# Leaving out identity products that TensorE runs while it waits

## The chip, the cores and the metric

One core of one Trainium2 chip runs the whole program. The metric is the device time of one execution in microseconds (us); the change is judged by the median over several executions. A profile is one further execution, recorded by the hardware profiler.

## What is computed

Two blocks of two layers each work on 256 tokens of width 1024, all in float32. The second block has an even layer (a recurrent mixer) and an odd layer (attention and a state-space part), and each of them ends in a mixture of experts, the part that the change touches:

```python
def hier_moe(h, w_group, b_group, w_expert, b_expert, w_gate, w_up, w_down):
    g_logits = (hf @ w_group + b_group).astype(jnp.float32)
    g_prob = jax.nn.softmax(g_logits, axis=-1)
    g_top = jnp.argmax(g_logits, axis=-1).astype(jnp.int32)
    ...
    top_p, top_j = lax.top_k(e_prob, MOE_TOP_K)
    gates = g_w[:, None] * top_p / jnp.sum(top_p, axis=-1, keepdims=True)
    expert_idx = g_top[:, None] * MOE_EXPERTS_PER_GROUP + top_j.astype(jnp.int32)
    y = routed_experts(hf, expert_idx, gates, w_gate, w_up, w_down)
```

There are 32 experts in 4 groups of 8. Each token takes its best group and the two best experts in it. An expert computes `(silu(x @ w_gate) * (x @ w_up)) @ w_down` with a hidden width of 512. No product of the identity with itself is part of any of this.

## The kernel before

**Layout.** The 256 tokens are two tiles of 128. The weights of all 32 experts are read from device memory in each of the two layers: 16 pairs of experts per layer, a pair in six pieces of 2 MB (four quarters of gate and up, two halves of down). A pair's products hold 32 slots per expert; four of these 32-column products lie side by side in TensorE's array.

**Routing** (class `Router`). TensorE transposes x (`x_transposes`, L2853) and forms the logits (`logits`, L2862). VectorE picks group and experts for one tile at a time (`select`, L2768 to L2778; its last instruction, L2778, raises `s_sel`). In `ranks` TensorE multiplies a triangular matrix and a matrix of ones with the selections, to give each token its slot (L2873, L2874, L2877, L2878, L2879; 32 columns each). VectorE makes the rank of a tile from that (L2806) and then the gathering matrix (L3078), which opens the experts.

**Experts** (`expert_functions`). For the first pair TensorE gathers x by quarters of the width (`gather_first`, L3168), VectorE scales what was gathered (L3100), and TensorE multiplies a quarter (`gate_up`, L3190). The first two gather quarters stand ahead of the first `gate_up`, and each of the other two stands behind one. In the steady loop `of_pair` one pair follows another: four `gate_up`, transposes, the gather of the next pair (L3157), a turn of the hidden values (L3227), two `down` (L3204), and the products that put the results back to their tokens (L3238). The last pair is written out in `of_last`.

**Loads.** SyncE issues every transfer into one queue, and before each one it waits until the buffer is free. The loads of the third pair (L2967) wait for `s_gu` of the first pair: when the first `gate_up` is through, the buffer of the first quarter may be filled again. In the even layer a half piece (`part_of`, L2710, 1 MB) goes out first on that signal, and the first whole piece on the signal of the second `gate_up`. In the odd layer a whole piece goes out on the first signal. What was issued ahead of that is limited: in the odd layer the last loads before routing ends are those at L2256 and one of 1 MB at L2710.

**The identity products.** `keep_clock(pe, n)` (L2841 to L2845) issues n products of the 128x128 identity with itself into bank 7, where nobody reads them. It waits for nothing and signals nothing. It is called at four places:
- in `ranks`, 5 products ahead of the wait for the second tile's selection (L2875), in both layers;
- in `ranks`, 2 products at its end (L2880), in both layers;
- in `of_last`, 4 products ahead of the first `down` of the last pair, in the odd layer only (L3278); the even layer has the products L3249 there, which it needs;
- at the end of the even layer's experts, 3 products (L3301), behind the first transposes of the odd layer (L425) and ahead of that layer's first products (L2512).

TensorE works through its instructions in program order. The profile shows two records for each float32 product, so 5 products are 10 records.

Of the kernel before, what the change touches and what calls it, by code (L numbers as in the profile page):

```python
# [13 lines left out]
P = 128  # L14
# [2639 lines left out]
class Router:  # L2654
# [183 lines left out]
        link(dve, dve.tensor_tensor(self.oh2, self.oh2, u2(c2(316)), ALU.mult))  # L2838
        link(dve, dve.tensor_tensor(self.gate, self.oh1, self.oh2, ALU.add))

    def keep_clock(self, pe, n):  # L2841

        ident = self.g.con("ident")
        for _ in range(n):
            pe.matmul(self.g.ps[7][:, 0:P], ident, ident, start=True, stop=True)  # L2845

    def x_transposes(self, pe, tt, ch):
        pe.wait_ge(self.s_x, 2 * tt + ch + 1)
        if tt:
            pe.wait_ge(self.s_xT, ch + 1)  # L2850
        for kk in range(4):
            k = 4 * ch + kk
            ins = pe.transpose(self.g.ps[6 + ch][:, kk * P:(kk + 1) * P], self.g.x[:, tt, k * P:(k + 1) * P], self.g.con("ident"))  # L2853
        ins.then_inc(self.s_tr, 1)
# [11 lines left out]
    def ranks(self, pe):  # L2866
        g, ps, sel = self.g, self.g.ps, self.sel
        before, ones = g.con("before"), g.con("ones")
        of_tile = lambda tt: ps[tt][:, 0:NE]
        pe.wait_ge(self.s_xT, 4)  # L2870
        pe.wait_ge(self.s_lo, 1)
        pe.wait_ge(self.s_sel, 1)
        pe.matmul(of_tile(0), before, sel[:, 0, :], start=True, stop=True).then_inc(self.s_rk, 1)  # L2873
        pe.matmul(of_tile(1), ones, sel[:, 0, :], start=True, stop=False)  # L2874
        self.keep_clock(pe, 5)  # L2875
        pe.wait_ge(self.s_sel, TT)
        pe.matmul(of_tile(1), before, sel[:, 1, :], start=False, stop=True).then_inc(self.s_rk, 1)  # L2877
        pe.matmul(ps[2][:, 0:NE], ones, sel[:, 0, :], start=True, stop=False)  # L2878
        pe.matmul(ps[2][:, 0:NE], ones, sel[:, 1, :], start=False, stop=True).then_inc(self.s_rk, 1)  # L2879
        self.keep_clock(pe, 2)  # L2880


class Experts:
# [6 lines left out]
def expert_functions(g, ly, c0, router):  # L2890
# [5 lines left out]
    ident = g.con("ident")  # L2896
# [255 lines left out]
    def tensor(pe):  # L3152
# [28 lines left out]
        def gate_up(quarter, where, bank, rounds):  # L3181
            if rounds is None:
                arrived_early(bank, quarter)
            else:
                arrived(bank, quarter, rounds)
            for k in range(2):
                for which in range(2):
                    for e in range(2):
                        q = (2 * which + e) * CAP
                        ins = pe.matmul(b_gu[q:q + CAP, :], xg[:, 2 * quarter + k, e * CAP:(e + 1) * CAP],  # L3190
                                        up_w(where, quarter, e)[:, which, k, :], start=(quarter == 0 and k == 0),
                                        stop=(quarter == 3 and k == 1), tile_position=(0, q))
            ins.then_inc(s_gu, 1)
# [59 lines left out]
        def of_last(pairs, rounds):  # L3253
            for quarter in range(4):
                if quarter % 2 == 0:
                    pe.wait_ge(s_xg, pairs * 2)
                gate_up(quarter, later[1], 1, rounds)
                if quarter < 3:
                    add_x(quarter)
            pe.wait_ge(s_P, pairs * 2)  # L3260
            for tt in range(TT):
                ins = pe.transpose(b_t[:, S + tt * P:S + (tt + 1) * P], Pg[:, tt].rearrange("p h e j -> p (h e j)"), ident)
            ins.then_inc(s_Pt, 1)
            pe.matmul(b_x[:, 0:1], ident, ident[:, 0:1], start=True, stop=True).then_inc(s_G, 2)
            pe.wait_ge(s_PTc, pairs)
            add_x(3)
            pe.wait_ge(s_h, pairs)
            for f in range(4):
                turn = pe.matmul if f == 0 else pe.transpose
                ins = turn(b_t[:, f * 2 * CAP:(f + 1) * 2 * CAP], hid[0:2 * CAP, f * P:(f + 1) * P],  # L3270
                           ident[0:2 * CAP, 0:2 * CAP])
            ins.then_inc(s_ht, 1)
            pe.wait_ge(s_xg, pairs * 2 + 2)
            pe.wait_ge(s_hc, pairs)
            if ly == 0:
                K_products(g.s5)
            else:
                router.keep_clock(pe, 4)  # L3278
            down(0, later[1], 1, rounds).then_inc(s_da, 1)
            down(1, later[1], 1, rounds).then_inc(s_dn, 1)  # L3280
            pe.wait_ge(s_yc, pairs)
            for tt in range(TT):
                for nh in range(2):
                    r = slice(nh * 2 * CAP, (nh + 1) * 2 * CAP)
                    pe.matmul(ps[2 * tt + nh][:, :], PT[r, tt * P:(tt + 1) * P], y[r, :], start=False, stop=True,  # L3285
                              skip_group_check=True).then_inc(s_sum[2 * tt + nh], 1)
# [11 lines left out]
        if ly == 0:  # L3298
            for ch in range(2):
                g.n_odd.transpose_half(pe, 0, ch)  # L3300
            router.keep_clock(pe, 3)  # L3301

    return sync, scalar, vector, tensor, gpsimd if ly == 0 else None


# [123 lines left out]
```

## Time and profile before

| | us |
|---|---|
| median of 3 runs | 1538.08 (1537.22 to 1539.68) |
| profiled execution, own time | 1537.3 |
| its span, first to last instruction | 1535.4 |
| TensorE busy | 1292.0 (84%) |
| VectorE busy | 462.7 (30%) |
| ScalarE busy | 278.2 (18%) |
| GpSimd busy | 266.0 (17%) |

The mean rate of the transfers is 324 GB/s over the span. The experts of the even layer run from about 538 to 970 us of the span, those of the odd layer from about 1104 us to the end. The page gives shares of engines over the span, and in its second part the span in 40 slices of 38.4 us with the granted clock of TensorE and what the DMA engines moved. Stages with different limits stand in one share, so the stretch around each edit has to be read by itself.

### The profile page before, as it was taken

How to read it: one execution, taken by the hardware profiler on the slowest of the kernel's cores; microseconds unless marked ns; L12 is line 12 of the kernel's file. 1: busy time of each engine (PE TensorE's matmuls, PEld its weight loads, DVE VectorE, ACT ScalarE, POOL GpSimd, SP SyncE). 2: the span in 40 equal slices, each digit the busy share in tenths (PEclk: the TensorE clock that was granted, in tenths of full speed). 3: DMA queues.
4: the chain of work that ended last, by engine and by line, in shares of the span. 5: the costliest groups of instructions: out<-in, count | busy, mean ns of one | idle time of the engine just before them, and what ended most of it. 6: DMA issues, size and time to landing. Idle time of an engine off the chain costs nothing. (4 is left out here: it accounts for less than half of the span.)

```text
span 1535.4 us, 21931 instructions
## 1 busy us (share of the span) xinstructions
PE 1292.0 (84%) x9264; PEld 698.4 (45%) x9264; DVE 462.7 (30%) x903; ACT 278.2 (18%) x547; POOL 266.0 (17%) x158
## 2 busy tenths in 40 slices
PE   9999999999999999667767667999998776676666
PEld 5754466547878554223223322755544232232232
DVE  2554662654845531111000101286311010010011
ACT  2042410423322210300000000115211101011011
POOL 0676226641000008790000000000000000000000
PEclk9999999999999999888889999999999888999999
DMA  9932452336430699999999999946799999999997
GB/s 371 359 127 82 182 227 84 140 138 271 183 139 31 255 416 423 428 432 433 428 433 426 436 429 427 394 166 241 275 424 431 428 435 430 427 434 430 427 436 300
DMA packets 36514, 498.18 MB, mean 324 GB/s; under 512 B 5728, under 2 KB 8544, under 8 KB 12256
## 3 DMA queue, kind: packets, MB, share of 16 engines
q1 hardware_dynamic: 36448, 497.22, 77.9%
q8 instruction: 51, 0.84, 0.2%
q14 instruction: 15, 0.12, 0.0%
HBM read 495.11 MB, written 2.10 MB: 324 GB/s over the span
## 5 line engine op out<-in xcount | busy, mean ns | idle before, releaser
L3190 PE MATMUL banks<-weight_ring,spare_weights_arena 128*32 128x512 f32 x1472 | 220.9, 751 | 143.9 <-DMA weight_ring<-in_moe_weights 142.4
L3111 DVE TENSOR_TENSOR spare_weights_arena<-spare_weights_arena,banks 64x512 f32<-64x512 f32 x32 | 22.1, 690 | 658.5 <-ACT spare_weights_arena L3030 658.5
L3190 PEld LDWEIGHTS banks<-weight_ring,spare_weights_arena 128*32 128x32 f32 x1472 | 56.4, 132 | 297.5 <-issue 244.6
L3157 PE MATMUL banks<-spare_weights_arena,x 128*128 128x64 f32 x960 | 110.8, 274 | 0.0
L3157 PEld LDWEIGHTS banks<-spare_weights_arena,x 128*128 128x128 f32 x960 | 109.9, 192 | 0.0
L3030 ACT ACTIVATE spare_weights_arena<-banks 64x512 f32<-64x512 f32 x32 | 18.9, 591 | 501.8 <-PE banks L3190 501.8
L3204 PE MATMUL banks<-weight_ring,spare_weights_arena 128*32 128x512 f32 x728 | 89.4, 624 | 13.9 <-issue 7.6
L1001 POOL TENSOR_TENSOR weight_ring<-spare_weights_arena,weight_ring 128x2048 f32<-128x2048 f32 x16 | 74.0, 4638 | 70.9 <-DVE spare_weights_arena L845 38.5
L1114 PE MATMUL banks<-weight_ring,x_normed_hT_mix 128*128 128x512 f32 x192 | 84.7, 592 | 0.0
L3238 PE MATMUL banks<-spare_weights_arena 64*128 64x512 f32 x240 | 59.6, 615 | 20.9 <-ACT spare_weights_arena L3036 20.9
L338 PE MATMUL banks<-weight_ring,x_normed_hT_mix 128*128 128x512 f32 x128 | 56.3, 595 | 0.0
L1082 PE MATMUL banks<-x_normed_hT_mix,weight_ring 128*128 128x256 f32 x256 | 56.0, 379 | 0.0
L3190 PE MATMUL banks<-x_normed_hT_mix,spare_weights_arena 128*32 128x512 f32 x272 | 36.7, 669 | 22.1 <-DMA x_normed_hT_mix<-in_moe_weights 22.1
L1114 PEld LDWEIGHTS banks<-weight_ring,x_normed_hT_mix 128*128 128x128 f32 x192 | 35.7, 190 | 41.4 <-issue 41.3
L3204 PEld LDWEIGHTS banks<-weight_ring,spare_weights_arena 128*32 128x32 f32 x728 | 25.7, 113 | 57.6 <-issue 37.1
L1082 PEld LDWEIGHTS banks<-x_normed_hT_mix,weight_ring 128*128 128x128 f32 x256 | 48.4, 190 | 7.6 <-issue 1.2
L1001 POOL TENSOR_TENSOR weight_ring<-weight_ring 128x512 f32<-128x512 f32 (+1 forms) x14 | 37.9, 2726 | 80.5 <-DMA weight_ring<-in_ring_weights 73.5
L3238 PEld LDWEIGHTS banks<-spare_weights_arena 64*128 64x128 f32 x240 | 20.6, 186 | 62.3 <-ACT spare_weights_arena L3036 48.1
L3092 DVE TENSOR_TENSOR spare_weights_arena<-banks,spare_weights_arena 128x256 f32<-128x256 f32 x64 | 27.0, 424 | 62.8 <-PE banks L3157 62.7
L3190 PE MATMUL banks<-spare_weights_arena 128*32 128x512 f32 x304 | 34.7, 595 | 12.9 <-DMA spare_weights_arena<-in_moe_weights 12.9
L3036 ACT COPY spare_weights_arena<-banks 128x512 f32<-128x512 f32 x32 | 18.8, 586 | 137.1 <-PE banks L3204 137.1
L1088 PE MATMUL banks<-weight_ring,x_normed_hT_mix 128*128 128x512 f32 x96 | 41.8, 593 | 0.2 <-DVE x_normed_hT_mix L415 0.2
(557 smaller groups left out, 1823.7 us busy)
## 6 DMA issues: line engine op xcount, KB each, us to landing
weight_ring<-in_moe_weights SPq DMA_DIRECT2D x42, 4096.0 KB, 26.9
weight_ring<-in_moe_weights SPq DMA_DIRECT2D x53, 2048.0 KB, 19.0
weight_ring<-in_ring_weights SPq DMA_DIRECT2D x35, 2048.0 KB, 12.2
spare_weights_arena<-in_moe_weights SPq DMA_DIRECT2D x21, 2048.0 KB, 51.5
x_normed_hT_mix<-in_moe_weights SPq DMA_DIRECT2D x16, 2048.0 KB, 54.8
spare_weights_arena<-in_moe_weights SPq DMA_DIRECT2D x7, 4096.0 KB, 54.5
weight_ring<-in_ring_weights SPq DMA_DIRECT2D x4, 1024.0 KB, 6.0
x_normed_hT_mix<-in_moe_weights SPq DMA_DIRECT2D x4, 1024.0 KB, 4.9
```

Of the source, the lines that this page charges most:

```text
L338: ins = pe.matmul(bank, lhsT[:, k, tt * P:(tt + 1) * P], w[:, k, n], start=(k == 0), stop=(k == k_all - 1))
L1001: sub = lambda out, left, right: pool.tensor_tensor(out, left, right, ALU.subtract)
L1082: ins = pe.matmul(bank[:, hh * S:(hh + 1) * S], w[:, k, h * P:(h + 1) * P], g.hT[:, k, :], start=(k == 0), stop=(k == KT - 1))
L1088: ins = pe.matmul(bank, g.hT[:, k, half * P:(half + 1) * P], w[:, k, :], start=(k == 0), stop=(k == KT - 1))
L1114: ins = pe.matmul(at_ps[n - 1], left[:, k, :], right[:, k, :], start=(n != P2 and k == 0), stop=(k == HT - 1), skip_group_check=n in (P1, P2))
L3030: act.activation(sil[0:2 * CAP, :], b_gu[0:2 * CAP, :], ACT.Silu).then_inc(s_sl, 1)
L3092: dve.tensor_tensor(xg[:, k, :], (b_x, b_dn)[h][:, 0:256].rearrange("p (k j) -> p k j", k=4), gcol[:, k].unsqueeze(2).to_broadcast([P, 4, ...
L3111: dve.tensor_tensor(hid[0:2 * CAP, :], sil[0:2 * CAP, :], b_gu[2 * CAP:4 * CAP, :], ALU.mult).then_inc(s_h, 1)
L3157: ins = pe.matmul((b_x, b_dn)[k // 4][:, k % 4 * 2 * CAP:(k % 4 + 1) * 2 * CAP], g.x[:, tt, k * P:(k + 1) * P], Pr[:, tt, :], start=(tt == ...
L3190: ins = pe.matmul(b_gu[q:q + CAP, :], xg[:, 2 * quarter + k, e * CAP:(e + 1) * CAP], up_w(where, quarter, e)[:, which, k, :], start=(quart ...
L3204: ins = pe.matmul(b_dn[q:q + CAP, :], hidT[:, 2 * half + f, e * CAP:(e + 1) * CAP], down_w(where, 4 + half, e)[:, f, nh * 512:(nh + 1) * 512],
L3238: pe.matmul(ps[2 * tt + nh][:, :], PT[r, tt * P:(tt + 1) * P], y[r, :], start=opens, stop=True, skip_group_check=True).then_inc(s_sum[2 * ...
```

## The change

`keep_clock` and its four calls are taken out: 7 products in each layer's routing, 4 at the end of the last pair, 3 ahead of the odd layer's first products, 21 in all (42 records). Nothing else differs.

```diff
@@ -2838,12 +2838,6 @@
-    def keep_clock(self, pe, n):
-
-        ident = self.g.con("ident")
-        for _ in range(n):
-            pe.matmul(self.g.ps[7][:, 0:P], ident, ident, start=True, stop=True)
-
@@ -2872,12 +2866,10 @@
         pe.matmul(of_tile(1), ones, sel[:, 0, :], start=True, stop=False)
-        self.keep_clock(pe, 5)
         pe.wait_ge(self.s_sel, TT)
         pe.matmul(of_tile(1), before, sel[:, 1, :], start=False, stop=True).then_inc(self.s_rk, 1)
         pe.matmul(ps[2][:, 0:NE], ones, sel[:, 0, :], start=True, stop=False)
         pe.matmul(ps[2][:, 0:NE], ones, sel[:, 1, :], start=False, stop=True).then_inc(self.s_rk, 1)
-        self.keep_clock(pe, 2)
@@ -3274,8 +3266,6 @@
             if ly == 0:
                 K_products(g.s5)
-            else:
-                router.keep_clock(pe, 4)
             down(0, later[1], 1, rounds).then_inc(s_da, 1)
@@ -3298,7 +3288,6 @@
                 g.n_odd.transpose_half(pe, 0, ch)
-            router.keep_clock(pe, 3)
```

On TensorE, in the odd layer's routing, before (L2862 logits, L2873 to L2879 ranks, L3168 the first gather, L3190 the first quarter of the first pair):

```order
L2862 MATMUL banks<-spare_weights_arena 128x48 x8
L2873 MATMUL banks<-spare_weights_arena,resident_constants 128x32
L2874 MATMUL banks<-spare_weights_arena,resident_constants 128x32
L2845 MATMUL banks<-resident_constants 128x128 x5
L2877 MATMUL banks<-spare_weights_arena,resident_constants 128x32
L2878 MATMUL banks<-spare_weights_arena,resident_constants 128x32
L2879 MATMUL banks<-spare_weights_arena,resident_constants 128x32
L2845 MATMUL banks<-resident_constants 128x128 x2
L3168 MATMUL banks<-spare_weights_arena,x 128x64 x8
L3190 MATMUL banks<-weight_ring,spare_weights_arena 32x512 x8
```

The same stretch after (lines ahead of the experts stand six lower, those in the experts eight lower):

```order
L2856 MATMUL banks<-spare_weights_arena 128x48 x8
L2867 MATMUL banks<-spare_weights_arena,resident_constants 128x32
L2868 MATMUL banks<-spare_weights_arena,resident_constants 128x32
L2870 MATMUL banks<-spare_weights_arena,resident_constants 128x32
L2871 MATMUL banks<-spare_weights_arena,resident_constants 128x32
L2872 MATMUL banks<-spare_weights_arena,resident_constants 128x32
L3160 MATMUL banks<-spare_weights_arena,x 128x64 x8
L3182 MATMUL banks<-weight_ring,spare_weights_arena 32x512 x8
```

Only the two rows L2845 are gone; between the logits and the first gather TensorE now has five products of 32 columns and the waits between them.

On TensorE, at the end of the last pair, before (L3242 adds x, L3270 turns the hidden values, L3204 is `down`, L3285 puts the results back) and then after:

```order
L3242 MATMUL banks<-x,resident_constants 128x512
L3270 MATMUL banks<-resident_constants,spare_weights_arena 128x64 x4
L3273 REGISTER_ALU
L2845 MATMUL banks<-resident_constants 128x128 x4
L3204 MATMUL banks<-spare_weights_arena 32x512 x16
L3285 MATMUL banks<-spare_weights_arena 128x512 x4
```

```order
L3234 MATMUL banks<-x,resident_constants 128x512
L3262 MATMUL banks<-resident_constants,spare_weights_arena 128x64 x4
L3265 REGISTER_ALU
L3196 MATMUL banks<-spare_weights_arena 32x512 x16
L3275 MATMUL banks<-spare_weights_arena 128x512 x4
```

The first `down` now stands right behind the turn of the hidden values.

## Rows read from the trace of the kernel before

**Rows 1.** The page: granted clock and transfers, span in 40 slices.

```profile
PEclk9999999999999999888889999999999888999999
DMA  9932452336430699999999999946799999999997
```

**Rows 2.** Identity products: records by engine, then busy us (xcount) in stretches.

```profile
L2845 PE MATMUL banks<-resident_constants x42: 275/275/356, 535.0 to 1521.4; 128*128 128x128 f32 x42
...
1100.00:1104.00 4.00, 2.05 (x14) 1.72 (x14) 1.00 0.97 410
```

**Rows 3.** Timeline, odd layer's routing: start, us, engine, what [idle before <-releaser].

```profile
1100.87 1.36 PE L2845 MATMUL banks<-resident_constants 128*128 128x128 f32 x10
...
1102.59 0.41 PE L2877 MATMUL banks<-spare_weights_arena,resident_constants 128*128 128x32 f32 x2 [0.35 <-DVE spare_weights_arena L2778]
...
1103.28 0.69 PE L2845 MATMUL banks<-resident_constants 128*128 128x128 f32 x4
1103.46 0.51 DVE L3078 TENSOR_SCALAR spare_weights_arena<-resident_constants,spare_weights_arena,small 128x32 f32<-128x32 f32 x2
...
1104.02 2.00 PE L3168 MATMUL banks<-spare_weights_arena,x 128*128 128x64 f32 x16
...
1106.80 1.92 PE L3190 MATMUL banks<-weight_ring,spare_weights_arena 128*32 128x512 f32 x16 [0.78 <-DVE spare_weights_arena L3100]
...
1108.78 18.04 SPq L2967 DMA_DIRECT2D weight_ring<-in_moe_weights  x6
```

**Rows 4.** Timeline of SyncE's queue, even layer: the first loads of the third pair.

```profile
542.91 0.33 SPq L2710 DMA_DIRECT2D weight_ring<-in_moe_weights  x1
...
545.80 13.51 SPq L2967 DMA_DIRECT2D weight_ring<-in_moe_weights  x5
```

**Rows 5.** Stretches: length, busy us PE, PEld, DVE, ACT, POOL; PEclk, DMA share, GB/s.

```profile
1105.00:1110.00 5.00, 4.22 (x38) 2.42 (x40) 1.91 (x11) 0.00 (x0) 0.00 (x0) 1.00 0.96 408
1110.00:1115.00 5.00, 5.00 (x48) 2.04 (x44) 2.20 (x11) 0.00 (x0) 0.00 (x0) 1.00 0.92 306
...
545.00:550.00 5.00, 5.00 (x48) 1.91 (x40) 2.90 (x16) 0.00 (x0) 0.00 (x0) 1.00 1.01 333
```

**Rows 6.** Stretches as above: routing, then two falls of the clock.

```profile
1100.00:1104.00 4.00, 3.25 (x25) 2.83 (x24) 3.58 (x22) 0.53 (x3) 0.00 (x0) 1.00 0.97 410
...
1118.00:1121.00 3.00, 2.65 (x24) 2.44 (x23) 1.86 (x5) 0.46 (x2) 0.00 (x0) 1.00 0.98 421
1121.00:1124.50 3.50, 3.34 (x16) 0.92 (x20) 0.58 (x2) 0.06 (x1) 0.00 (x0) 0.51 1.01 431
...
717.50:721.50 4.00, 1.07 (x12) 0.13 (x4) 0.00 (x0) 0.00 (x0) 0.00 (x0) 1.00 0.97 414
721.50:725.00 3.50, 3.45 (x17) 0.59 (x17) 0.00 (x0) 0.00 (x0) 0.00 (x0) 0.53 1.02 435
```

**Rows 7.** Timeline of TensorE: like waits for a piece, and the group behind.

```profile
1223.26 3.46 PE L3190 MATMUL banks<-x_normed_hT_mix,spare_weights_arena 128*32 128x512 f32 x16 [2.97 <-DMA x_normed_hT_mix<-in_moe_weights]
...
1340.10 3.32 PE L3190 MATMUL banks<-x_normed_hT_mix,spare_weights_arena 128*32 128x512 f32 x16 [2.96 <-DMA x_normed_hT_mix<-in_moe_weights]
...
1398.54 1.92 PE L3190 MATMUL banks<-x_normed_hT_mix,spare_weights_arena 128*32 128x512 f32 x16 [2.97 <-DMA x_normed_hT_mix<-in_moe_weights]
```

**Rows 8.** Timeline, end of the last pair.

```profile
1520.53 1.13 PE L2845 MATMUL banks<-resident_constants 128*128 128x128 f32 x8 [0.55 <-ACT spare_weights_arena L3034]
...
1525.18 1.92 PE L3204 MATMUL banks<-spare_weights_arena 128*32 128x512 f32 x16 [1.68 <-DMA spare_weights_arena<-in_moe_weights]
...
1527.81 1.99 PE L3285 MATMUL banks<-spare_weights_arena 64*128 64x512 f32 x8 [0.70 <-ACT spare_weights_arena L3036]
```

**Rows 9.** Timeline, start of the odd layer.

```profile
970.44 1.28 DVE L431 TENSOR_TENSOR x_normed_hT_mix<-banks,spare_weights_arena 128x512 f32<-128x512 f32 x2
970.56 0.75 PEld L2845 LDWEIGHTS banks<-resident_constants 128*128 128x128 f32 x6
...
971.33 3.74 PE L2512 MATMUL banks<-x_normed_hT_mix,weight_ring 128*128 128x128 f32 x32
```

## The prediction

> **What bounds the kernel now.** I read the page's slices first [rows 1]. In both stretches of experts the DMA engines are busy in every slice, and TensorE's granted clock dips in some. A core that waits for weights there pays for whatever interrupts the stream of transfers, and for nothing else until the last piece has landed. Outside them TensorE itself is the limit. The second look is at the four places of the edit, in the timeline, with the question who is waited for on either side of the identity products. The third is at the queue of transfers just behind routing. It asks how much of it is left when the first `gate_up` of a layer frees a buffer. The last is at the clock: what TensorE did before the stretches in which the profile shows half of it (1.2 GHz, against 2.4).
>
> **The instructions that go, by themselves.** 42 records go; 14 of them cover 2.05 us of TensorE in one routing [rows 2]. Almost none of that is on the path.
> - Routing, five products: they run from 1100.87 to 1102.23, and the next product starts at 1102.59, behind VectorE's selection of the second tile [rows 3]. Gone, they leave a longer wait. Worth 0.
> - Routing, two products: they end at 1103.97, as does VectorE's gathering matrix (L3078, 1103.46 plus 0.51), for which the gather at 1104.02 waits [rows 3]. Worth 0; below 0.1 at best. In the even layer all this looks the same.
> - Last pair, four products: the first `down` starts some 1.1 us earlier, but the second waits for its piece until 1525.18 with or without them [rows 8]. Worth 0 as long as nothing else changes. The wait ahead of it grows from 1.68 to 1.68 + 1.13 = 2.8 us.
> - Odd layer, three products: the hidden half that L2512 needs first is the first of two VectorE operations of 1.28 us together from 970.44, so there by about 971.1, while L2512 starts at 971.33 [rows 9]. A gain between 0 and 0.2; I take 0.1.
>
> So, if the clock stays, the sum is -0.1 us, nothing that can be measured.
>
> **What they cover: the clock.** In routing the profile shows full clock and TensorE busy 3.25 of 4 us; without the 2.05 us of L2845 that is 1.2 of 4 [rows 2, 6]. Two rows tell what happened elsewhere after thin work. From 717.5 to 721.5 TensorE was busy 1.07 of 4 us, and in the stretch behind it the granted clock was 0.53. From 1118 to 1121 it was busy 2.65 of 3 us, with products of 64 columns (L3157, L3227) and hardly a wait, and the clock still fell, to 0.51 from 1121 to 1124.5 [rows 6]. Routing without the identity products is thinner than either of these in what goes through the array: products of 32 columns and waits. The likeliest reading is that the clock falls in both layers, somewhere between the end of the logits and the first gather, and stays low while the gather's narrow products follow; it comes back behind wide products of the first pair, as it did behind the wide groups in these rows.
>
> The Trainium skill speaks against this at first sight: "TensorE: Matmul & The Clock Gate", under "HAM oscillation", makes the rule one of long idle gaps of TensorE, and routing has none. By that rule the clock stays and the time is that of the first rival below. The fall at 1121 came behind work without such a gap [rows 6], so I give the rule little weight.
>
> **What half clock costs, odd layer.** The gather takes 2.00 us from 1104.02, then TensorE waits 0.78 for VectorE, and the first quarter's 16 records take 1.92 from 1106.80 [rows 3]. At half clock the gather takes 4.0, so the quarter starts 4.0 - 2.00 - 0.78 = 1.2 us later. A group of 16 wide records took 3.46 and 3.32 us where the clock was low, against 1.92 [rows 7]: 1.5 more. The buffer is freed 2.7 us later; 2.0 if the clock returns halfway through the group. I take 2.5. Does the queue hide it? SyncE issues the next load at 1108.78, right behind that group [rows 3], and from 1110 to 1115 the transfers ran at 306 GB/s, against 408 in the five before [rows 5]. The queue is already running out there: 5 x (1 - 306/408) = 1.25 us of transfer are lost in the kernel before. It has no reserve, so the whole 2.5 goes to the stream, which is full from there to the last piece. **Odd layer: 2.5 us**, from 1.2 (some reserve left) to 2.8.
>
> **Even layer.** The same delay of 2.5 us at the first signal, which brings only 1 MB (542.91); the first whole piece comes with the second signal, 2.9 us later (545.80) [rows 4]. The rate fell to 333 GB/s from 545 to 550, less than in the odd layer [rows 5], and the DMA share stayed at 1.01. Two small pieces overlap here, so I allow a reserve of 0.9 us. **Even layer: 1.6 us**, from 0.5 to 3.5 (if the second quarter also runs at half clock). The delay comes out at the layer's end, where TensorE again waits for the last piece.
>
> **Last pair.** A wait of 2.8 us has its nearest neighbours in four waits of 2.96 to 2.98 us for a piece (three of them in [rows 7], the fourth at 1281.67). Behind three the group of 16 took 3.3 to 3.5 us, behind the fourth 1.92. So two chances in three that the final `down` takes 1.5 us more, with all that follows behind it [rows 8]. **1.0 us** as its share; 0 and 2.0 are the ends.
>
> **Sum.** -0.1 + 2.5 + 1.6 + 1.0 = +5.0 us. The profiled execution took 1537.3 us (span 1535.4, 1.9 around it), so its like after should be 1542.3; the median before is 1538.08, which gives **1543.1 us**. A measurement of this kernel can tell some 0.2%, 3.1 us, from no change; 5.0 is above that, though not by much.
>
> **Rivals.**
> - *The clock stays in routing.* The products only fill waits, and the time is 1538.08 - 0.1 = 1538.0, or 1539 with the last wait. For it: no single wait in routing is longer than about 1.6 us. Against it: the fall at 1121. This is also the case in which the change does nothing. Chance 0.13.
> - *The clock falls, but the queue hides most of it.* Transfers move no later than before by more than 1 us in each layer: 1538.08 + 1 + 0.5 = 1539.6. For it: the DMA share is 0.92 and 1.01 in the thin stretches, never near 0. Against it: the rates 306 and 333 GB/s. It decides if the load behind the first `gate_up` has more than 2 us to spare. Chance 0.10.
> - *The clock stays low through the second quarter too*, and the next loads come late as well: 2.8 + 3.5 + 2.0 = 8.3, so 1546.4. Chance 0.07.
> - *Faster.* The identity products and their 128-column weight loads stand in TensorE's queue ahead of work that is ready: the rank product at 1102.59, the gather, the first `down`. If each of these starts 0.5 us earlier in both layers and the stream follows, the time is 1538.08 - 2 x 1.0 - 0.2 = 1535.9. Against it: at all these places VectorE or a transfer ends last [rows 3, 8]. Between 0.2% and nothing lies most of its chance; it decides only if the clock stays. Chance 0.03.
> - *The forecast*, two delayed layers, 1541 to 1545: chance 0.67.
>
> **How the numbers follow.** The forecast and the rival with the long fall give slower by over 0.2%, save for the forecast's lower edge (1541.1 is 3.0 above): 0.67 + 0.07 - 0.03 = 0.71. Within 0.2%: 0.13 + 0.10 + 0.03 for that edge, and 0.01 of the faster rival: 0.27. Faster: the other 0.02. The range of 8 in 10 has to reach into the second rival and leave out the first and part of the third: 1538.8 to 1545.9.
>
> **What would show it.** In the profile after, the granted clock between 1100 and 1110 us and at the same place of the even layer should read about 0.5, the gather should take near 4 us, and the first load behind it should be issued some 2.5 us later than 1108.78. The rate in the five us behind that should fall below 306 GB/s. If the clock reads 1.00 there, the forecast is wrong at its root; if it reads 0.5 and the last piece still lands on time, the queue had a reserve that I didn't see. The last `down` should take 3.3 us or 1.92, and the time of single executions may scatter by that difference.

## The result and the profile after

| | before | after |
|---|---|---|
| median of 9 executions, us | 1537.22 (1534.91 to 1539.68) | 1541.18 (1539.02 to 1543.41) |
| ratio, 95% interval | | 1.0024 (1.0012 to 1.0035) |
| profiled execution, us | 1537.3 | 1541.15 |
| its span, us | 1535.4 | 1539.3 |
| mean granted clock | 0.951 | 0.929 |

The changed kernel is 4.0 us slower, for 42 fewer records on TensorE. A second comparison, with 11 executions against 33, gave 1.0017 (1.0008 to 1.0026); both are clear of no change.

The stretches behind routing, in the profile after (columns as in rows 5 and 6: length, busy us of PE, PEld, DVE, ACT and POOL, granted clock, DMA share, GB/s), even layer first:

```profile
535.00:540.00 5.00, 3.85 (x17) 3.72 (x18) 4.50 (x27) 1.59 (x3) 0.00 (x0) 0.50 0.98 419
540.00:545.00 5.00, 5.00 (x26) 1.99 (x25) 0.62 (x3) 0.00 (x0) 0.00 (x0) 0.54 0.94 394
545.00:550.00 5.00, 5.00 (x48) 2.53 (x51) 1.43 (x7) 0.00 (x0) 0.00 (x0) 1.00 0.87 291
...
1106.00:1111.00 5.00, 5.00 (x24) 3.71 (x28) 2.53 (x14) 0.00 (x0) 0.00 (x0) 0.50 0.97 415
1111.00:1116.00 5.00, 5.00 (x28) 2.38 (x24) 0.29 (x1) 0.00 (x0) 0.00 (x0) 0.50 0.64 221
```

The granted clock is half (1.2 GHz) through both gathers and both first groups. The same places in before had 1.00 [rows 5, 6]. From 1111 to 1116 the DMA engines were busy for 0.64 of the time and moved 221 GB/s; in before the dip was 306 [rows 5]. In the even layer it is 291 where before had 333.

The timeline of the odd layer's routing, after (start, us, engine, line, what [idle before <- releaser]; L2870 was L2877 before, L3160 was L3168, L3182 was L3190):

```profile
1104.31 0.61 PE L2870 MATMUL banks<-spare_weights_arena,resident_constants 128*128 128x32 f32 x2 [1.55 <-DVE spare_weights_arena L2778]
...
1105.82 3.68 PE L3160 MATMUL banks<-spare_weights_arena,x 128*128 128x64 f32 x16
...
1109.42 3.64 PE L3182 MATMUL banks<-weight_ring,spare_weights_arena 128*32 128x512 f32 x16
...
1113.13 17.07 SPq L2959 DMA_DIRECT2D weight_ring<-in_moe_weights  x5
```

The gather took 3.68 us against 2.00, the first group 3.64 against 1.92 [rows 3]. VectorE's last selection releases L2870 at 1104.31, as it released L2877 at 1102.59; counted from there, the first group starts 0.9 us later (5.11 against 4.21) and the first load goes out 2.6 us later (8.82 against 6.19).

The end of the last pair, after (L3196 was L3204, L3275 was L3285):

```profile
1522.11 1.92 PE L3196 MATMUL banks<-spare_weights_arena 128*32 128x512 f32 x16 [0.51 <-ACT spare_weights_arena L3026]
...
1526.82 2.90 PE L3196 MATMUL banks<-spare_weights_arena 128*32 128x512 f32 x16 [2.79 <-DMA spare_weights_arena<-in_moe_weights]
...
1530.40 3.79 PE L3275 MATMUL banks<-spare_weights_arena 64*128 64x512 f32 x8 [0.69 <-ACT spare_weights_arena L3028]
```

The wait is 2.79 us instead of 1.68, and the last down and the last products take 1.0 and 1.8 us more than in [rows 8]: here the clock fell behind the wait.

The start of the odd layer shows the small gain: from VectorE's first operation to L2512 it is 0.83 us (972.16 to 972.99), and in [rows 9] it is 0.89.

```profile
972.16 1.28 DVE L431 TENSOR_TENSOR x_normed_hT_mix<-banks,spare_weights_arena 128x512 f32<-128x512 f32 x2
...
972.99 3.25 PE L2512 MATMUL banks<-x_normed_hT_mix,weight_ring 128*128 128x128 f32 x27 [0.44 <-DVE x_normed_hT_mix L431]
```

The two profiles add up like this. The even layer's last down starts 432.96 us after its first rank product, and 430.62 in before: +2.3. In the odd layer the same distance is 424.66 against 424.75: -0.1. From the start of the last down to the last copy of x it is 8.1 against 5.3: +2.7. Behind that copy the output goes out, and the span ends 4.3 us later against 4.9: -0.5, so of the fall at the last pair 2.2 us reach the end. The stretches ahead of routing differ by 0.6 us in favour of after, and no edit touches them. Together that is the 3.9 us between the two spans. The clock fell in the three places where that was foretold, yet the odd layer's delay is nowhere at its end. That is what the experiments had to settle.

### The profile page after: what moved, and what is told of

Its sections match the earlier page's. It is cut to its first block, busy times and chain, and to the rows that moved or that the text cites. A ratio compares the mean times of both kernels' runs of the same rounds, so it can differ in the third digit from the quotient of the medians.

```text
span 1539.3 us, 21847 instructions
## 1 busy us (share of the span) xinstructions
PE 1317.0 (86%) x9222; PEld 714.9 (46%) x9222; DVE 458.9 (30%) x903; ACT 278.7 (18%) x547; POOL 267.1 (17%) x158
## 4 chain that ended last, share of the span: by engine, by line
PE 43%; DMA 24%; another core or an unknown queue 4%; DVE 2%; ACT 1%; issue 1%; SPq 0%; DVEq 0%
DMA weight_ring<-in_moe_weights 21%; PE banks L3182 13%; PE banks L3196 5%; PE banks L3149 4%; PE banks L338 3%; DMA x_normed_hT_mix<-in_moe_weights 3%; PE banks L3230 2%; PE banks L1792 2%; PE banks L1985 2%; PE banks L2605 2%; PE banks L2512 1%; PE banks L3160 1%; PE banks L1333 1%; PE banks L1917 1%
## 5 line engine op out<-in xcount | busy, mean ns | idle before, releaser
L3182 PE MATMUL banks<-weight_ring,spare_weights_arena 128*32 128x512 f32 x1472 | 217.3, 741 | 120.8 <-DMA weight_ring<-in_moe_weights 120.8
L3182 PEld LDWEIGHTS banks<-weight_ring,spare_weights_arena 128*32 128x32 f32 x1472 | 54.0, 130 | 271.5 <-issue 221.6
L3149 PE MATMUL banks<-spare_weights_arena,x 128*128 128x64 f32 x960 | 124.4, 294 | 0.0
L3149 PEld LDWEIGHTS banks<-spare_weights_arena,x 128*128 128x128 f32 x960 | 123.9, 212 | 0.0
L3196 PE MATMUL banks<-weight_ring,spare_weights_arena 128*32 128x512 f32 x728 | 93.5, 648 | 16.3 <-issue 7.6
L1114 PE MATMUL banks<-weight_ring,x_normed_hT_mix 128*128 128x512 f32 x192 | 84.7, 592 | 0.0
L3196 PEld LDWEIGHTS banks<-weight_ring,spare_weights_arena 128*32 128x32 f32 x728 | 26.7, 117 | 64.1 <-issue 44.4
L338 PE MATMUL banks<-weight_ring,x_normed_hT_mix 128*128 128x512 f32 x128 | 56.3, 596 | 0.0
L3182 PE MATMUL banks<-x_normed_hT_mix,spare_weights_arena 128*32 128x512 f32 x272 | 35.5, 649 | 20.6 <-DMA x_normed_hT_mix<-in_moe_weights 20.6
L3196 PE MATMUL banks<-spare_weights_arena 128*32 128x512 f32 x280 | 39.8, 693 | 8.9 <-DMA spare_weights_arena<-in_moe_weights 4.8
L3182 PE MATMUL banks<-spare_weights_arena 128*32 128x512 f32 x304 | 36.4, 620 | 11.4 <-DMA spare_weights_arena<-in_moe_weights 11.4
```

Source lines behind the costliest of these rows:

```text
L338: ins = pe.matmul(bank, lhsT[:, k, tt * P:(tt + 1) * P], w[:, k, n], start=(k == 0), stop=(k == k_all - 1))
L1114: ins = pe.matmul(at_ps[n - 1], left[:, k, :], right[:, k, :], start=(n != P2 and k == 0), stop=(k == HT - 1), skip_group_check=n in (P1, P2))
L3149: ins = pe.matmul((b_x, b_dn)[k // 4][:, k % 4 * 2 * CAP:(k % 4 + 1) * 2 * CAP], g.x[:, tt, k * P:(k + 1) * P], Pr[:, tt, :], start=(tt == ...
L3196: ins = pe.matmul(b_dn[q:q + CAP, :], hidT[:, 2 * half + f, e * CAP:(e + 1) * CAP], down_w(where, 4 + half, e)[:, f, nh * 512:(nh + 1) * 512],
```

## The experiments

Each kernel has 11 or 12 executions against 33 or 35 of before on the same chip. Spreads in brackets behind a median are those of single executions.

### One place at a time

**e1_even_routing**: only the even layer's routing loses its seven products.

```diff
-        self.keep_clock(pe, 5)
+        if self.ly:
+            self.keep_clock(pe, 5)
...
-        self.keep_clock(pe, 2)
+        if self.ly:
+            self.keep_clock(pe, 2)
```

> The seven identity products are left out of the even layer's routing alone; the other places keep theirs. Theory of the clock: the granted clock reads 0.50 from the wait for the second selection to the first group of the first pair, that group ends 2.5 to 2.7 us later than before, the loads of the third pair go out that much later, and the stream of transfers carries it to the end: +2.3 us (the last down of the even layer came 2.3 us later in the changed kernel, counted from routing). Rival, the products only fill waits: the clock reads 1.00 and the time is unchanged within 0.3 us. Rival, the queue hides it: clock 0.50, last piece of the even layer on time, 0 to +0.5 us.

Median 1538.16 us against 1538.37, ratio 1.0002 (0.9994 to 1.0011). The profile shows half clock in the even layer, as foretold, and the last down of the layer 432.85 us after its first rank product: 2.2 us more than in the profile of before. The interval, -0.9 to +1.7 us, leaves that out. Mechanism seen, full price not seen; the section on the prediction comes back to it.

**e2_odd_routing**: the same in the odd layer (`if self.ly == 0:`).

> The seven identity products are left out of the odd layer's routing alone. The forecast put +2.5 us here. In the changed kernel's profile the first load behind the first group went out 2.6 us later than before, counted from routing, and the bytes of the stream ran some 1.3 us behind, but the last piece landed no later. Theory that the stream carries it: +1.3 to +2.5 us. Rival that the last transfer to finish does not feel the gap (some of the 16 DMA engines had work left while others idled): clock 0.50 in routing, first load late by 2.6 us, and the time within +0.5 us.

Median 1537.41 us, ratio 0.9994 (0.9985 to 1.0003). Half clock in the odd layer's routing, the first group 1.9 us later, the last down 423.51 us after the first rank product. No cost can be told. By itself this speaks for the rival that the end of the stream does not feel the gap.

**e3_last_pair**: only the four products ahead of the last pair's first down go.

```diff
-            else:
-                router.keep_clock(pe, 4)
```

> The four identity products are left out ahead of the last pair's first down, in the odd layer, alone. Theory of the clock: the wait for the last piece grows from 1.7 to 2.8 us; in some executions the clock falls behind it and the last down and the products that put the results back take together up to 2.7 us more (in the changed kernel: down 2.90 us instead of 1.92, the last products 3.79 instead of 1.99), in others not. The median moves by +1 to +2 us, and the executions scatter more than those of before. Rival, the products fill a wait and nothing else: 0, with the scatter of before.

Median 1538.21 us, ratio 1.0005 (0.9994 to 1.0016), spread 1536.4 to 1544.7. In this profile the wait was again 2.79 us and the clock held behind it:

```profile
1527.67 1.92 PE L3204 MATMUL banks<-spare_weights_arena 128*32 128x512 f32 x16 [2.79 <-DMA spare_weights_arena<-in_moe_weights]
1530.30 1.99 PE L3283 MATMUL banks<-spare_weights_arena 64*128 64x512 f32 x8 [0.70 <-ACT spare_weights_arena L3036]
```

The same profile held the surprise of the study. Routing has all its identity products here, but in the odd layer the clock fell all the same (stretches of TensorE alone):

```profile
1100.00:1104.00 4.00, 3.63 (x31) 0.95 1.00 393
1104.00:1108.00 4.00, 4.00 (x21) 0.50 1.00 426
...
1111.08 3.25 PE L3190 MATMUL banks<-weight_ring,spare_weights_arena 128*32 128x512 f32 x16
```

The five products themselves ran mostly at half clock there (2.33 us against 1.36), and the first group ended 11.4 us after the first rank product, later than in the profiles that leave them out (10.2 to 10.9). The kernel before is not a kernel whose clock always holds: where routing kept its products, in 3 of 8 passes through it the clock fell before the first group was through.

**e4_odd_start**: only the three products ahead of L2512 go (`router.keep_clock(pe, 3)` at the end of `tensor`).

> The three identity products are left out ahead of the odd layer's first products alone. Every theory expects next to nothing: -0.1 us (the first product starts behind VectorE 0.06 us sooner in the changed kernel), and the clock stays at 1.00, as wide weight loads and 128-column products stand on both sides. Rival: their place matters for the clock, and it reads 0.50 somewhere from 966 to 990 us: +1 to +3 us.

Median 1537.76 us, ratio 1.0001 (0.9990 to 1.0012). No fall between 966 and 990 us. The interval, -1.5 to +1.8 us, tells no worth of these three.

### All gone, routing gone, thin products, more products

**f1_all_gone** is the changed kernel.

> The changed kernel itself once more, on the chip and in the rounds of the three beside it. Taken one place at a time the removals gave +0.3, -0.9, +0.8 and +0.2 us, each uncertain by some 1.4 us and none told from no change, while all together had given +3.7 (1.8 to 5.4). Theory of the clock: +2.5 to +4.5 us again, with half clock in both routings. Rival, the first comparison was high by chance: within +1.5 us.

Median 1541.40 us against 1538.77, ratio 1.0017 (1.0008 to 1.0026). The cost is there again: 2.6 us by the medians, after 4.0 in the first comparison.

**f2_routing_both**: both `keep_clock` calls in `ranks` go, the other two stay.

> The seven identity products are left out of routing in both layers; those ahead of the last down and ahead of the odd layer's first products stay. Forecast's terms: +2.5 and +1.6, so +4.1 us. After the runs with one layer each: the even layer's share is what the stream carries (2.25 us in a profile, against a kernel that itself falls in some executions), the odd layer's is small; +1 to +2.5 us. If it equals the run with all gone, the last pair costs nothing.

Median 1538.66 us (1538.37 to 1541.95), ratio 1.0010 (1.0001 to 1.0019). Its mean is 2.2 us below that of f1_all_gone, each mean uncertain by about 1 us, so the last pair costs at least about as much as both routings, once measured beside them.

**f3_thin**: all 21 products stay, but stream one column.

```diff
-            pe.matmul(self.g.ps[7][:, 0:P], ident, ident, start=True, stop=True)
+            pe.matmul(self.g.ps[7][:, 0:1], ident, ident[:, 0:1], start=True, stop=True)
```

> All 21 identity products stay in their places, but each streams one column of the identity instead of 128 (the 128-column weight load stays), so TensorE executes as many instructions over nearly the same time and next to nothing goes through the array. If what holds the clock is what the products put through the array: half clock in both routings and the time of the kernel with all gone, within 1 us. Rival, that TensorE only has to be executing something: clock 1.00 there and the time of before.

Median 1539.62 us, ratio 1.0012 (1.0003 to 1.0021). The odd layer's routing (timeline, then stretches of TensorE alone; the very last line is of before, at the same place as the first stretch):

```profile
1102.57 1.25 PE L2845 MATMUL banks<-resident_constants 128*128 128x1 f32 x10
...
1106.44 3.65 PE L3168 MATMUL banks<-spare_weights_arena,x 128*128 128x64 f32 x16
...
1100.00:1104.00 4.00, 3.46 (x31) 1.00 0.94 397
1102.00:1106.00 4.00, 3.41 (x22) 0.75 1.00 426
1106.00:1110.00 4.00, 4.00 (x19) 0.50 0.98 418
...
1098.30:1102.30 4.00, 3.57 (x31) 1.00 0.95 397
```

TensorE executes as many instructions over nearly the time of before (1.25 us against 1.36 for ten records), busy 3.46 of 4 us up to the fall against 3.57 at the same place of before, and here the clock falls. It fell in both layers, as in the kernels without these products. Two passes are few, since with full products it fell in 3 of 8; but together with the time, which is above that of before beyond its interval, they speak against the rival that TensorE only has to be executing something.

The time lies 1.8 us below that of all gone, outside the 1 us that was expected. One difference is seen: the last pair stayed at full clock in the one profile, behind a wait of 1.79 us. That this is all of the 1.8 us is not shown.

**f4_more** puts in more of them where TensorE waits anyway.

```diff
+        self.keep_clock(pe, 1)
         pe.wait_ge(self.s_xT, 4)
...
-        self.keep_clock(pe, 5)
+        self.keep_clock(pe, 6)
...
+            if rounds is None:
+                for _ in range(2):
+                    pe.matmul(b_gu[:, 0:P], ident, ident, start=True, stop=True)
             pe.wait_ge(s_xg, n * 2 + 4)
...
         gather_first(1)
+        router.keep_clock(pe, 3)
```

> More identity products than before, at places where TensorE waits anyway: one ahead of the first rank product, six instead of five ahead of the second selection, three between the first gathers and the first gate_up, and two ahead of the first down of each of the first three pairs, in both layers. In two of the profiles that keep all of routing's products the clock still fell in or right behind routing, in others not. Theory: the kernel before pays for such falls in some executions, this one in fewer; median -0.5 to -2 us against before and less scatter, the clock 1.00 from routing to the third pair. Rival: the kernel before has its scatter from elsewhere (the transfers), 0; and if the additions are not hidden, +1 us.

Median 1536.09 us (1535.80 to 1537.67), ratio 0.9986 (0.9977 to 0.9995): faster than both kernels. Its spread is 1.9 us against 5.7 of before beside it (1535.65 to 1541.35), though of 11 executions against 33. Its profile has full clock through both routings:

```profile
1100.00:1104.00 4.00, 3.79 (x31) 1.00 0.99 418
1104.00:1108.00 4.00, 3.89 (x35) 1.00 1.02 438
...
1106.95 0.89 PE L2845 MATMUL banks<-resident_constants 128*128 128x128 f32 x6
...
1107.90 1.92 PE L3191 MATMUL banks<-weight_ring,spare_weights_arena 128*32 128x512 f32 x16
```

So the kernel before seems to pay for falls of its clock in part of its executions. The mean granted clock doesn't show it: it is 0.943 over the executions of either kernel, and f4_more's profile has 0.944 without any fall in routing, so most of the half clock lies elsewhere, in the streams. Against f4_more the changed kernel is 1541.4 - 1536.1 = 5.3 us slower by the medians, side by side, and 4.8 by the two ratios.

### A delay without the clock

The next four build on f4_more, which was not measured again beside them: they are compared with it by their ratios to before, each uncertain by 0.0009 or so.

**g1_late_even** and **g2_late_odd** put ten more products ahead of the first `gate_up` of one layer, so that it comes late at full clock.

```diff
-        router.keep_clock(pe, 3)
+        router.keep_clock(pe, 13 if ly == 0 else 3)
```

> Base is the kernel with more identity products (1536.1 us median in its own comparison, ratio 0.9986 to before), whose clock holds in routing. In the even layer alone, ten further identity products stand ahead of the first gate_up: it comes some 2.3 us late (ten products of 0.23 us) at full clock, so the delay of the stream is measured without a fall. If the stream has no reserve there, +2.3 us against the base (ratio to before about 1.0001); with the reserve of 0.9 us that the forecast allowed, +1.4; if the queue hides it, 0 (ratio 0.9986).

> The same in the odd layer alone: ten further identity products ahead of its first gate_up, 2.3 us at full clock. The forecast said the queue has no reserve there: +2.3 us against the base. The profiles so far speak for some: the last piece landed 424.7, 424.5 and 424.1 us after routing where the first group ended 10.9 us after it, 424.8 and 423.3 where it ended at 8.3. So 0 to +0.8 us by that reading.

| | g1_late_even | g2_late_odd |
|---|---|---|
| median, us | 1538.56 (1536.64 to 1539.87) | 1535.94 (1535.29 to 1538.98) |
| ratio to before | 1.0004 (0.9994 to 1.0013) | 0.9992 (0.9983 to 1.0001) |
| above the base's ratio | 0.0018, 2.8 us | 0.0006, 0.9 us |

The additions delay the first group by 2.1 us in each layer (8.47 us from rank product to group, 6.37 in the base). Timelines of g1_late_even, the even layer's first group and its last down, and of g2_late_odd the same in the odd layer:

```profile
543.13 1.92 PE L3191 MATMUL banks<-weight_ring,spare_weights_arena 128*32 128x512 f32 x16
...
967.44 1.07 PE L3205 MATMUL banks<-weight_ring,spare_weights_arena 128*32 128x512 f32 x8 [0.48 <-DMA weight_ring<-in_moe_weights]
...
1108.14 1.92 PE L3191 MATMUL banks<-weight_ring,spare_weights_arena 128*32 128x512 f32 x16
...
1523.30 1.06 PE L3205 MATMUL banks<-spare_weights_arena 128*32 128x512 f32 x8 [1.67 <-DMA spare_weights_arena<-in_moe_weights]
```

In the even layer the last down starts 432.78 us after the first rank product, and 430.55 to 431.06 in the four profiles of this base or the routing-only one that delay nothing there: +1.7 to +2.2 of 2.1. The delay arrives whole, and no fall of the clock is in it. In the odd layer it is 423.63, within the 422.21 to 423.64 of its undelayed relatives: 0.6 us above their mean, anything from 0 to 1.4. The two intervals overlap at the ends, so the medians alone would not prove the difference; the distances in the profiles carry it.

Where the delay enters the stream is seen in what the transfers moved. The first column begins at the layer's first rank product (GB/s; once full, the stream moves 427 to 431):

| | first 20 us | from 40 to 60 us |
|---|---|---|
| even: before | 403 | 416 |
| even: f4_more | 406 | 410 |
| even: g1_late_even | 392 | 379 |
| even: after | 387 | 381 |
| odd: before | 395 | |
| odd: f4_more | 408 | |
| odd: g2_late_odd | 381 | |
| odd: after | 365 | |

The four stretches of 20 us of before and after, and the four microseconds of the even layer in which its queue runs out a second time (length, granted clock, DMA share, GB/s), before first in each pair:

```profile
574.56:594.56 20.00, 0.94 1.01 416
573.95:593.95 20.00, 1.00 0.94 381
...
578.56:582.56 4.00, 1.00 0.92 373
577.95:581.95 4.00, 1.00 0.63 197
...
1100.43:1120.43 20.00, 1.00 0.98 395
1102.16:1122.16 20.00, 0.66 0.91 365
```

At some 430 GB/s the even layer's stream in after is 0.7 us behind before's at the end of the first stretch and takes another 1.6 us in the second: 2.4 in all, for a first buffer 2.6 us late. In g1_late_even it is 0.7 and 1.4 against f4_more. So most of the even layer's price arises in a second thin place, some 45 us behind the first rank product. The odd layer has none: from 20 to 60 us its rate is 428 to 430 in all four. Its stream is 1.3 us behind in g2_late_odd against f4_more, of 2.1, and 1.4 in after against before, of 2.6. The queue hides about 1 us of either delay.

**g3_more_no_last**: the base without the four products of the last pair.

> The same base, with the four identity products ahead of the last pair's first down left out. All gone against routing alone gone gave +2.2 us on the mean, the last pair alone against before +0.8. If the wait of 2.8 us makes the clock fall in part of the executions: +1 us on the mean against the base and more scatter, with one group of executions near the base and one 2 to 3 us above. If the last pair costs nothing by itself: 0, scatter as the base.

Median 1537.47 us (1536.46 to 1539.20), ratio 1.0002 (0.9993 to 1.0011), so 0.0016 or 2.5 us above the base's ratio, uncertain by some 2 us. The profile shows one fall in full:

```profile
1522.54 3.10 PE L3205 MATMUL banks<-spare_weights_arena 128*32 128x512 f32 x16 [2.78 <-DMA spare_weights_arena<-in_moe_weights]
1526.33 3.78 PE L3287 MATMUL banks<-spare_weights_arena 64*128 64x512 f32 x8 [0.69 <-ACT spare_weights_arena L3037]
```

From the start of the last down to the last copy it took 8.3 us, against 5.3 in all profiles where the clock held. To the end of the span it is 12.6 against 10.2, so 2.4 us of the fall reach the end. Two separate groups of executions, as expected, can't be made out; the spread is wider than the base's, but not in two lumps.

**g4_routing_more**: the base without the two products ahead of the first pairs' downs.

> The same base without the two products ahead of the first down of the first three pairs: only routing has more (one, six, and three ahead of the first gate_up). It tells where the gain of the base comes from. If falls in routing alone cost the kernel before its time: as the base, 1536 us. If falls behind the first pairs' gathers (as at 1121 us of the profile before) count as well, between the base and before: 1537 to 1538 us.

Median 1536.84 us (1534.71 to 1540.61), ratio 0.9989 (0.9979 to 1.0000). The median lies by the base's, the spread by before's. It doesn't separate the two readings.

### The profiles side by side

Distances in us, each from the first rank product of the layer. "Group" is the end of the first group of 16 records, "down" the start of the last down. The last column goes from the start of the odd layer's last down to the end of the last copy of x.

| profile | even: group, down | odd: group, down | last |
|---|---|---|---|
| before | 8.3, 430.6 | 8.3, 424.8 | 5.3 |
| e4_odd_start | 8.3, 430.5 | 9.7, 422.9 | 5.3 |
| f4_more | 8.3, 431.1 | 8.3, 423.3 | 5.3 |
| g3_more_no_last | 8.3, 430.6 | 8.3, 423.1 | 8.3 |
| g4_routing_more | 8.3, 430.6 | 8.3, 423.6 | 5.3 |
| g1_late_even | 10.4, 432.8 | 8.3, 422.2 | 5.3 |
| g2_late_odd | 8.3, 430.6 | 10.4, 423.6 | 5.3 |
| e1_even_routing | 10.4, 432.9 | 8.3, 423.4 | 5.3 |
| e2_odd_routing | 8.3, 432.1 | 10.2, 423.5 | 5.3 |
| e3_last_pair | 10.0, 433.8 | 11.4, 424.7 | 5.3 |
| f2_routing_both | 10.9, 433.2 | 10.9, 424.5 | 5.3 |
| f3_thin | 10.4, 432.4 | 11.5, 424.7 | 5.3 |
| after | 10.9, 433.0 | 10.9, 424.7 | 8.1 |
| f1_all_gone | 10.9, 435.1 | 10.9, 424.1 | 6.9 |

Even layer: a group 1.7 to 2.6 us late puts the last down 1.8 to 3.2 us late, and once 4.5. e2_odd_routing has its group on time and the down 1.5 us late; its clock fell at 555 us instead, in the first pair. The two largest delays, e3_last_pair and f1_all_gone, had a further fall some 41 to 45 us behind the first rank product, just ahead of the second thin place: 82 and 90 GB/s in its four microseconds, where after has 197.

Odd layer: with a group up to 2.1 us late the last down starts at 422.9 to 423.6, about as it does without a delay (422.2 to 423.6), and with 2.6 to 3.2 us it starts at 424.1 to 424.7, about 1.2 us later than the 423.3 of f4_more. The profile of before is the exception, 424.8 with a group on time, and it is the one from which the forecast was made. It has a fall at 1121 us [rows 6], in the first pair, 20.7 us behind the first rank product, as e2_odd_routing's at 555 is. It spread the first six loads of L2967 over 18.04 us [rows 3], where f4_more has 16.47:

```profile
1109.88 16.47 SPq L2968 DMA_DIRECT2D weight_ring<-in_moe_weights  x6
```

The rates behind it show no loss from that, though, so the fall doesn't explain the 424.8. Its stream was 0.6 us behind that of f4_more; the rest lies in the tail of the last piece, below.

## Why the prediction was right

1543.1 was forecast, with 1538.8 to 1545.9; measured are 1541.18 and 1541.40. Slower by over 0.2% had 0.71, and the ratios are 1.0024 and 1.0017, one on each side of that bound. The mechanism was right: the clock falls, the first buffer comes free late, and the end of the layer or the last pair pays. That the sum came so near is in part luck, since one term was too large and two were too small. By the steps of the prediction:

**The products by themselves are worth nothing.** Nothing speaks against it: -0.06 us at the odd layer's start, no measurable gain at e4_odd_start.

**The clock falls in both layers.** Held in every one of the profiles that left routing's products out, eight passes of eight, against three of eight where before's products stand. f3_thin, two passes of two, makes it likely that the columns they stream matter and not that TensorE is busy. The rule of the Trainium skill ("TensorE: Matmul & The Clock Gate", "HAM oscillation") would have left the clock alone in routing, whose longest wait after the change was 1.55 us. Here the measurement differs from it.

**Half clock frees the first buffer 2.5 us late.** Measured 2.6 in each layer, counted from the first rank product.

**Odd layer, 2.5 us to the end.** This term was too large. The first load went out 2.6 us late and the rate dipped to 221 GB/s, as the forecast said, but the last piece came 0 us late against before and about 1.2 against f4_more. The failing step is "it has no reserve", read from one dip in the rate: of 2.6 us the stream took on only 1.4 (365 against 395 GB/s over 20 us). The rest of the difference to before is at its end. The tail of the last piece in before and after (stretches of 1 us, clock, DMA share, GB/s):

```profile
1520.00:1521.00 1.00, 1.00 0.89 377
1521.00:1522.00 1.00, 1.00 0.51 197
1522.00:1523.00 1.00, 1.00 0.27 115
1523.00:1524.00 1.00, 1.00 0.15 66
1524.00:1525.00 1.00, 1.00 0.04 16
```

```profile
1523.00:1524.00 1.00, 1.00 1.04 442
1524.00:1525.00 1.00, 1.00 0.57 229
1525.00:1526.00 1.00, 1.00 0.31 131
1526.00:1527.00 1.00, 1.00 0.00 0
```

In before the full rate ends at about 1521 and a few DMA engines work on for some 4 us; in after it ends some 3 us later, and the tail is 2 us long. Against f4_more the last down of before comes 1.4 us later with its stream 0.6 behind, and that of after 1.3 later with its stream 2.0 behind. So the profile from which the forecast was made had a long tail, and that hides in it what the stream passed on. Why the tail differs from one execution to the next no view shows; that stays open.

**Even layer, 1.6 us.** Too small; it measured 2.3 in the profile after. The reserve that the forecast allowed is there right behind routing, and larger than 0.9 us: the stream lost 0.7 of 2.6 us there. What failed is the assumption behind both layers that the stream is full from there on. The even layer's queue runs out a second time at some 580 us, and there it lost 1.6 us more. g1_late_even shows the same at full clock.

**Last pair, 1.0 us.** Two chances in three were foretold, where the forecast's own rows had three falls in four waits; the clock fell in 3 of the 4 profiles that have the long wait. What one fall costs was too small as well: 1.5 was taken from the down alone, but in two of the three the last products also run at half clock. It came to 2.2, 1.5 and 2.4 us at the end of the span (after, f1_all_gone, g3_more_no_last). The share should have been 1.5.

**The base.** The kernel before has falls of its own. Its one profile shows one at 1121 us, which the forecast used as a sign that thin work loses the clock, and for which it put no price on the base. How much that is can be estimated from the table. In the even layer the last down starts at 430.6, 430.5, 432.1 and 433.8 in the four profiles that keep routing's products there as in before, 431.8 on the mean, and at 433.5 in the four without: +1.8. In the odd layer the means are 424.0 and 424.2: +0.2. With the last pair's 1.5 and -0.1 that is 3.4 us, where 4.0 and 2.6 were measured. It is an estimate from four profiles each, made after the fact. It also removes most of the trouble with e1_even_routing: against the mean of its kind its even layer is 1.1 us late and not 2.2, and 1.1 lies inside its interval. Against a kernel that holds the clock the terms are 2.3 + 1.2 + 1.5 - 0.1 = 4.9 us, and f1_all_gone is 4.8 to 5.3 above f4_more. The forecast of 5.0 was thus nearly the distance to a kernel that holds its clock, and too high against the kernel before.

## What to carry to other kernels

Work that fills waits and computes nothing may still hold TensorE's clock; before it goes, look at what runs next at half clock and who waits for that. A filler that keeps TensorE busy is not by that alone a filler that holds the clock: here one-column products did not, in two passes of two. Where a kernel loses its clock in some executions, one profile is one draw: compare the granted clock at the same place in several, and look for falls in the kernel before too, since they are already in its time. A dip in the transfer rate shows that a stream has run dry, but not how much of a further delay it passes on. To price it, sum what was moved over the stretch, look further down the stream for a second dip, or delay the first release on purpose and look at the last landing.

## What the runs showed of the hardware

- With one-column products and full-width weight loads TensorE was busy 3.46 of 4 us ahead of a fall to 1.2 GHz (f3_thin, odd layer; it fell in the even one too); with as many 128-column products, busy 3.57 of 4 at the same place (before), it held 2.4 GHz in 5 of 8 passes.
- With equal instructions and nearly equal times, the clock falls in one execution and not in another: 3 of 8 passes through the unchanged routing, 3 of 4 waits of 2.8 us at the end.
- A delay of 2.1 us at the head of a stream of some 180 MB (420 us at about 430 GB/s) arrived in full after 430 us in the even layer (1.7 to 2.2 us), and about 0.6 us of it in the odd layer (0 to 1.4).
